# Four more modulation blocks summed on VectorE during the key and value projections

## What is computed

```
mod_x = silu(c) @ w_mod + b_mod          # 2048 -> 6*2048: sh1, sc1, ga1, sh2, sc2, ga2
hx = modulate(rmsnorm(x), sh1, sc1);  hc = the same of the context with its own vector
px = hx @ w_in;  pc = hc @ w_in          # conv channels, q, sigmoid(o), k, v, gates
m_lat  = mlstm_bidir(pc, px, ...)        # 4 heads of 256, forward and backward
cv_lat = conformer_conv(px, ...)         # depthwise conv of 31 taps, LayerNorm, silu
x = x + ga1 * (concat(m_lat, cv_lat) @ w_out)
x = x + ga2 * peer(modulate(rmsnorm(x), sh2, sc2), ...)
```

## Time and profile before

| | us |
|---|---|
| median of 3 runs | 3466.61 |
| lowest, highest | 3463.43, 3469.53 |
| the profiled execution | 3474.34 |
| its span in the trace | 3472.5 |
| PE busy | 3390.8 (98%) |
| DVE / POOL / ACT busy | 2290.6 / 1802.3 / 1013.9 |

### The profile page before, as it was taken

One profiled execution on the slowest core, in us unless ns is written; L12 is line 12 of the kernel. 1 busy time (PEld: TensorE's weight loads), 2 busy tenths in 40 slices (PEclk: granted clock), 3 DMA queues, 4 the chain that ended last, 5 costly groups with the idle time before them and its releaser, 6 DMA issues.

```text
span 3472.5 us, 44870 instructions
## 1 busy us (share of the span) xinstructions
PE 3390.8 (98%) x17051; PEld 2939.8 (85%) x17051; DVE 2290.6 (66%) x3784; ACT 1013.9 (29%) x1163; POOL 1802.3 (52%) x904
## 2 busy tenths in 40 slices
PE   6999999999999999999999999999999999999998
PEld 3688888756788889999999999999888888888886
DVE  2288886224514569994787887864667676777666
ACT  3332211143323223223322222223233233232333
POOL 1220000211544446667666666667777777777764
PEclk8999999999999999999999999999999999999999
DMA  8756642157424226777677777778988888888872
GB/s 333 282 180 204 217 147 98 67 219 307 196 104 152 86 106 237 266 271 279 260 304 308 273 283 313 302 305 309 380 333 322 323 326 324 318 329 320 322 278 97
DMA packets 177717, 874.70 MB, mean 252 GB/s; under 512 B 15865, under 2 KB 76745, under 8 KB 88896
## 3 DMA queue, kind: packets, MB, share of 16 engines
q1 hardware_dynamic: 115248, 525.37, 41.5%
q0 software_dynamic: 38688, 281.15, 20.0%
q10 hardware_dynamic: 23664, 66.69, 5.0%
HBM read 803.78 MB, written 69.32 MB: 251 GB/s over the span
## 4 chain that ended last, share of the span: by engine, by line
PE 88%; DVE 7%; DMA 2%; POOL 1%; issue 1%; ACT 1%; ACTq 0%; DVEq 0%; SPq 0%; POOLq 0%
PE bank L2011 82%; PE bank L2257 2%; PE bank L2373 1%; DMA ring<-in_w_mod 1%; PE bank L2229 1%; PE bank L2019 1%; DVE b L1776 1%; DVE rows_a L1715 1%; DVE b L1756 0%; DVE low L1356 0%; DMA low<-k 0%; DVE rows_c L1715 0%; PE bank L2357 0%; DVE tiny L1771 0%; DVE rows_b L1715 0%
## 5 line engine op out<-in xcount | busy, mean ns | idle before, releaser
L789 POOL TENSOR_TENSOR split<-ring,split 128x1024 fp32r<-128x1024 f32 x544 | 1303.1, 2409 | 543.5 <-ACT split L1099 541.6
L2011 PE MATMUL bank<-h_hi,split 128*128 128x384 f32 (+1 forms) x4608 | 1221.8, 341 | 8.2 <-POOL split L789 6.9
L1099 ACT ACTIVATE split<-ring 128x1024 fp32r<-128x1024 f32 x544 | 577.6, 1062 | 1609.3 <-PE bank L2011 1598.9
L2011 PE MATMUL bank<-split,a_split 128*128 128x512 f32 x4608 | 1045.0, 389 | 0.1
L2011 PEld LDWEIGHTS bank<-split,a_split 128*128 128x128 f32 x4608 | 865.1, 188 | 179.7 <-POOL split L789 0.5
L2011 PEld LDWEIGHTS bank<-h_hi,split 128*128 128x128 f32 x4608 | 839.2, 188 | 29.6 <-POOL split L789 8.8
L2011 PE MATMUL bank<-h_lo,split 128*128 128x384 f32 (+1 forms) x2304 | 785.3, 341 | 0.0
L1893 DVE TENSOR_TENSOR acc<-acc,bank 128x512 f32<-128x512 f32 x372 | 251.4, 683 | 289.9 <-PE bank L2011 288.9
L2011 PEld LDWEIGHTS bank<-h_lo,split 128*128 128x128 f32 x2304 | 433.7, 188 | 9.4
L2011 PE MATMUL bank<-hT_hi,w_hi 128*128 128x512 f32 (+1 forms) x768 | 289.7, 377 | 8.6 <-DVE hT_lo L1361 4.6
L2011 PE MATMUL bank<-hT_lo,w_hi 128*128 128x512 f32 (+1 forms) x768 | 287.5, 374 | 0.0
(11 more groups left out here) (302 smaller groups left out, 3732.7 us busy)
## 6 DMA issues: line engine op xcount, KB each, us to landing
ring<-in_u_emb SPq DMA_DIRECT2D x128, 1024.0 KB, 4.8
ring<-in_v_emb SPq DMA_DIRECT2D x128, 1024.0 KB, 4.9
ring<-in_w_mod SPq DMA_DIRECT2D x64, 1024.0 KB, 8.6
ring<-in_w_in SPq DMA_DIRECT2D x44, 1024.0 KB, 4.9
ring<-in_w_mod SPq DMA_DIRECT2D x64, 512.0 KB, 4.5
neurons<-tiny ACTq DMA_DIRECT2D x128, 192.0 KB, 3.0
gate_table<-b ACTq DMA_DIRECT2D x6, 4096.0 KB, 14.7
weigh<-neurons SPq DMA_DIRECT2D x32, 768.0 KB, 8.2
```

The source lines that it names most:

```text
L789: nc.gpsimd.tensor_tensor(split[:, r % 2, 1, at].bitcast(F32R), ring[:, r % 4, :, :].rearrange("p k n -> p (k n)")[:, at], split[:, r % 2, ...
L1099: nc.scalar.activation(split[:, q % 2, 0, at].bitcast(F32R), ring[:, q, :, :].rearrange("p k n -> p (k n)")[:, at], ACT.Copy)\
L2011: last = mm(out_, left[a].bitcast(F32R), right[b].bitcast(F32R), start=start and n == 0, stop=stop and n == 2)
```

## The change

A constant `SUMMED` = 12 comes beside `PAIRED` = 8. Rows blocks 8 to 11 (quarters `r` = 32 to 47) leave PE and are summed by DVE in `sum_late`, now into four SBUF places (`late_acc`) instead of PSUM, at three points of the LayerNorm and gate work: two quarters after the first reduction, four after the second, ten after the clears of the gates' tiles. Their loads are interleaved with the weight loads on SP. `mean_late` adds up the partitions on PE after unit 46; `store_late` on ACT copies and stores the four rows. The heads keep blocks 12 to 15: block 12 around the scores of head 0, three quarters of block 13 after it, the last quarter before the numerators of head 0, block 14 before those of head 1, block 15 after those of head 2.

```
+SUMMED = 12
...
+            late, weight = 4 * PAIRED, 4 * PAIRED + 6
+            for halves, weights in ((1, 4), (1, 1), (1, 2), (4, 1), (3, 1), (3, 1), (3, 0)):
+                for _ in range(halves):
+                    row_halves(late)
+                    late += 1
+                for _ in range(weights):
+                    in_load(weight)
+                    weight += 1
...
+            def sum_late(r):
+                b, q = r // 4, r % 4
+                acc = late_acc[b - PAIRED]
+                for kk in range(QT):
+                    if kk % 2 == 0:
+                        dve.wait_ge(row_full[kk // 2], 16 * (r + 1))
+                    factor = c_silu[:, q * QT + kk:q * QT + kk + 1]
+                    if q == 0 and kk == 0:
+                        nc.vector.tensor_scalar(acc, ring[:, 3, kk, :], factor, None, ALU.mult).then_inc(row_added, 1)
+                        continue
+                    dve.wait_ge(row_added, 4 * r + kk)
+                    nc.vector.scalar_tensor_tensor(acc, ring[:, 3, kk, :], factor, acc, ALU.mult, ALU.add)\
+                        .then_inc(row_added, 1)
...
             for kind in range(2):
                 nc.vector.memset(grow[2 + kind], 0.0).then_inc(gate_clear, 1)
+            for r in range(38, 48):
+                if r == 40:
+                    dve.wait_ge(spill_stored, 16 * 7)
+                sum_late(r)
...
+            def mean_late():
+                pe.wait_ge(row_added, 16 * SUMMED)
+                pe.wait_ge(gate_nat, 2)
+                for b in range(4):
+                    last = mm(bank[32 * b:32 * b + 32, 7, :], mean_w[:, 0:32], late_acc[b], start=True, stop=True,
...
                     last.then_inc(quarter_used, 1)
+                    if r == KV_R + 14:
+                        mean_late()
...
-            row_block(9)
+            row_block(13, ROW_ORDER[0:3])
             for h in range(HEADS):
                 if h + 1 < HEADS:
                     head_scores(h + 1)
-                    row_block(10 + 2 * h)
+                if h == 0:
+                    row_block(13, ROW_ORDER[3:])
+                if h == 1:
+                    row_block(14)
...
-                if h + 1 < HEADS:
-                    row_block(11 + 2 * h)
+                if h == 2:
+                    row_block(15)
```

More of the change, by code:

```diff
@@ L81 @@
 MOD2 = (22, 23, 23, 8)
-WO = tuple(n + 8 for n in MOD2)
+WO = tuple(n + 16 - SUMMED for n in MOD2)
 WQ = tuple(n + 4 for n in WO)
@@ L560, in _ @@
                 in_load(r + 6)
-            for r in range(4 * PAIRED + 6, WO_R):
-                in_load(r)
+            late, weight = 4 * PAIRED, 4 * PAIRED + 6
[6 more added lines that the diff above has]
+                    weight += 1
             def row_load(b, q):
-                if b > PAIRED:
+                if b > SUMMED:
                     sp.wait_ge(quarter_used, rows_used_up(b - 1, q))
@@ L584, in _ @@
             qk_load(0)
-            row_load(8, ROW_ORDER[3])
-            for b in range(9, 16):
-                for q in ROW_ORDER:
-                    row_load(b, q)
-                if b in (9, 10, 12):
-                    qk_load((9, 10, 12).index(b) + 1)
-                if b == 9:
-                    sp.wait_ge(spill_stored, 16 * 8)
-                if b in (9, 10, 12, 14):
-                    v_load_head((9, 10, 12, 14).index(b))
+            row_load(12, ROW_ORDER[3])
+            qk_load(1)
+            for q in ROW_ORDER:
+                row_load(13, q)
+            sp.wait_ge(spill_stored, 16 * 8)
+            v_load_head(0)
+            qk_load(2)
+            for q in ROW_ORDER:
+                row_load(14, q)
+            v_load_head(1)
+            qk_load(3)
+            v_load_head(2)
+            v_load_head(3)
+            for q in ROW_ORDER:
+                row_load(15, q)
             sp.wait_ge(gate_dve, 9)
@@ L972, in empty_kv @@
                 spilled(4 + n)
+                if n == 3:
+                    act.wait_ge(mrow_stored[0], 16 * 2)
                 if n == 1:
@@ L1092, in _ @@
                         last.then_inc(w_made, 1)
-                for b in (8 + 2 * h, 9 + 2 * h):
-                    copy_row(b, 4 if b == 8 else 6 + b % 2, row_buf_c)
+                copy_row(12 + h, 4 if h == 0 else 6 + h % 2, row_buf_c)
             def hi_half(q, h):
@@ L1466, in _ @@
                 .then_inc(ln_step, 1)
+            dve.wait_ge(mrow_stored[1], 16)
+            for r in range(32, 34):
+                sum_late(r)
             dve.wait_ge(pass_full, 1)
@@ L1473, in _ @@
                 .then_inc(ln_step, 1)
+            for r in range(34, 38):
+                sum_late(r)
             dve.wait_ge(ln_std_made, 1)
@@ L2208, in _, with row_block @@
             pe.wait_ge(kv_free, 18 + BANK_ORDER.index(4) + 1)
-            def row_block(b):
-                if b >= 10:
-                    pe.wait_ge(mrow_made, b - 7)
-                for q in ROW_ORDER:
+            def row_block(b, order=ROW_ORDER):
+                if b >= 14:
+                    pe.wait_ge(mrow_made, b - 10)
+                for q in order:
                     row_unit(b, q, 6 + b % 2)
```

50 lines of the change are left out of this document (32 added, 18 removed).

## The result

The changed kernel takes 3474.4 us (median of 13 runs; eleven lie between 3472.3 and 3476.0, two at 3465.0 and 3466.6) against 3466.6 us before (13 runs, 3462.2 to 3469.5): a ratio of 1.0021, interval 1.0012 to 1.0029. It is 0.2% slower. The forecast was 3462.3 us with a range to 3473.5, so the sign missed, and the range by 0.9 us.

A forecast was written before the change was run, and what follows sets the result against it. PE carries the chain of waits, so work taken off it counts only where nothing else makes it wait. Heads -7.3, mean matmuls +1.0, wait for sums +2.0: -4.3 from 3466.6 gives 3462.3 us, range 3454.5 to 3473.5.

The forecast's parts named there:

- (f): Key and value projections: DVE's 64 sums, without POOL's delay, end at 712, leaving PE 14 us of room.
- (b): Heads, from head 0's scores' end to its numerators: -6.3 us, bounds -8.8 and -4.8; the wait for a quarter goes.
- (c): Heads, before head 2's numerators: the rows block there goes, -3.57 us.
- (d): Gaps of 3.3 us behind numerators of heads 0 and 1: low clock afterwards costs 1.3 us each, +2.6, bounds 0 and +5.4.
- Heads in all: Sum of the forecast terms for the heads: -6.3 - 3.6 + 2.6 = -7.3 us.
- (e): Key and value projections: the matmuls of `mean_late` add 1.0 us to PE, all on the path.
- (g): POOL's weight splits stretch DVE's two-input sums: end at 728, PE waits +2.0 us, bounds 0 and +12.
- (f) or (g) was undersized: Sign to look for: PE idle over 6 us before `mean_late` means the sums' time or POOL's delay was set too small.
- the slow rival: PE stands at `mean_late` until the last sum; at 738 it waits 12 us plus some 2 us low clock: 3474; 16%.
- the sums are late: POOL's splits and DMA latency delay DVE's sums; decides from an end at 732.4; +7.7 us, 3474; chance 16%.
- Weights late: Row loads on SP hold up weight units, ACT's split is late, PE waits in unit 46 or 47: 3468 to 3476; 3%.

The follow-up runs named there:

- e_place: Changed kernel with rows blocks 13, 14, 15 moved behind the numerators of heads 0, 1, 2, block 14's loads behind v's: 3459.0 us, 0.9980 of the kernel before.
- e_fill: Changed kernel plus four unused matmuls on PE behind the numerators of head 0 and of head 1: 3474.2 us, ratio 1.0019 to the kernel before.
- after2: Second trace of the changed kernel, nothing altered: 3479.0 us for the one traced execution.
- after4: Fourth trace of the changed kernel, nothing altered: 3459.1 us for the one traced execution.
- e_nolow: Changed kernel with POOL writing zeros instead of computing the weights' low parts for units 43 to 47: 3463.2 us, ratio 0.9990 to the kernel before.
- e_slices: Changed kernel with late quarters loaded as four slices of 256 KB instead of two halves: 3465.4 us, ratio 0.9994 to the kernel before.

## Why the prediction was wrong, step by step

The step that failed is (f), the time of the sums without POOL, and beside it a term that the sum put at nothing, the restart behind PE's wait. (f) came out 7.8 us too early, which made the wait 6.7 us instead of 2.0; the restart cost 2.5. These two turn the sign in the traces, from -4.3 to +2.7. They don't explain the time in full: 3466.6 + 2.7 is 3469.3 us, inside the range, and what took the median on to 3474.4 stays open.

- **(b)** -6.3 forecast, 27.6 - 22.4 = -5.2 measured, inside its bounds. "The waiting for the quarter goes" was wrong: 3.9 us of it stayed. `m` starts 8.8 us after the scores' end (773.81 - 765.03); in e_place, where it waits for ACT's Exp alone, 6.9 (769.98 - 763.04). So 1.8 us of the wait was not covered.
- **(c)** -3.57: right. The numerators of head 2 start at 854.56, with the end of the scores.
- **(d)** +2.6 forecast, +0.6 and +0.5 measured, e_fill as a check. The place and the sign were right, the cover by the copies was underrated. Nor does the clock fall each time: in after2 and after4 it falls behind one of the two gaps of 3.3 us.
- **Heads in all**: -7.3 forecast; -7.4, -4.2, -7.6 and -10.8 in four traces against 155.6. Right in size in the first trace by luck, as the errors of (b) and (d) partly cancel. The scatter wasn't foreseen.
- **(e)** 1.0: right.
- **(f)** failed. The quarter's period without POOL was taken as 5.6 us; in e_nolow the last seven quarters take 672.5 to 716.0, 6.2 us each, and all ten (716.0 - 655.6) / 10 = 6.0, with a wait of 3.54 us for v's store among them (2 allowed). The quarters ahead of the reciprocal were to end at 646.5, 58.8 us after the reduction's start; without the splits they end at 61.9. In all the sums without POOL end 132.1 us after that start, where (f) had 712 - 587.7 = 124.3: 7.8 us too early. The latencies came from a quieter stretch: at 145 to 154 us of before the DMA engines move 117 GB/s, at 655.6 to 716 us of e_nolow 236. That this made them longer is likely but no run isolates it; the bound of 5 us, which was written down "because weights and v's store are on the way", was nearer than the value taken.
- **(g)** had the right mechanism (e_nolow) and was over-sized: from 712 to 728 = 16 us forecast, 12.9 measured. One piece of evidence in it was misread: the reciprocal of 3.35 us was called stretched by POOL, and 2.6 us were to come back. It takes 3.35 us alone too [e_nolow, 645.82]; nothing came back. The prediction's own sign, a wait of over 6 us for "(f) or (g) was undersized", came true, for (f).
- Together the sums end 145.0 us after the start instead of 140.3: 4.7 us late, and PE arrives at 721.6 as forecast (138.3 us after the start against 138.4). So the wait is 6.7 us and not 2.0. With no slack left, every microsecond of error in a chain of 64 sums goes into the time at full price, while room of 6 us (e_nolow: PE is there at 722.16, the sums at 716.0) would have hidden it.
- **The restart behind the wait** is missing from the sum: 2.5 us of low clock in the mean and unit 47. It was in the slow rival only ("some 2 us more"), as if it came with a long wait alone. The Trainium skill ("TensorE: Matmul & The Clock Gate", section "HAM oscillation — how this bites in real kernels") tells of a kernel that waits for DMA between its bursts of matmuls, and there every burst starts at the low clock. The rows at 0.51 behind the 6.70 us, a wait for DVE here, agree; the scores behind the 3.31 us in after2, at full pace, do not. The prediction used the rule for the heads but not here.
- The sum by the measured terms is -5.2 - 3.6 + 1.1 + 1.0 + 6.7 + 2.5 = +2.5, and the two traces show +2.7; as the 2.5 is itself what remains of the 10.2, this checks the heads' terms only. The rival "the sums are late" was the right one. Its decision point, 732.4 in before's times, is where the sums did end (728.3 + 4.4 = 732.7); one outcome can't judge its chance of 16%, but its own working named 732 for the slower latencies.
- **Weights late** (3%): ACT got unit 47 at 707.07 after 8.05 us for its DMA, 1.6 us after PE had freed the place. No PE wait came of it, but the split moved with it and lay on the sums.

## What to carry to other kernels

Work that is moved to an engine with much idle time becomes a chain with its own end. Add up that chain with the latencies of the stretch in which it will run, and take the slow row, when another engine waits for its last link. A wait put into PE costs itself and, in most rows here, the low clock behind it; a block of matmuls is free only in a gap that something else ends, so look for those gaps first (e_place) and count what the waits in front of them cost if they stay empty. And a load that is split finer, so that each place is refilled while its neighbours are used, freed PE here as fully as removing the contention did.

## What the hardware showed

How far POOL holds up DVE depends on what POOL does. Five subtractions that read SBUF (4.6 to 4.9 us each) delayed the chain of sums by 12.9 us in all; with five writes of zeros of the same size (1.8 us each) in their place, the sums of two SBUF inputs beside them kept their 1.54 us a pair. The Trainium skill ("SBUF — State Buffer", section "SBUF: two separate sides") has it so for operations with two SBUF inputs, against a GpSimd operation that reads SBUF; the runs agree. The first sum of each block is of another kind: it reads one SBUF tensor and a factor, so not all the new sums read two, as was said ahead of the prediction. It was caught as well, in e_slices inside the split that starts at 691.35 (0.48 us elsewhere), and a little beside the zeros (0.85 us in e_nolow):

```profile
691.80 4.85 DVE L1463 TENSOR_SCALAR top<-ring,c_silu 128x512 f32<-128x512 f32 x1
```

And the same program can differ from itself by 11 us in a stretch of 310 us (307.4 to 318.6 in four traces), by when a chain of DVE, POOL and DMA lets PE go on, by one operation of DVE inside or ahead of a split, and by the clock behind short waits. The kernel before, where PE waits for none of these sums, repeats within 0.5 us in three.
